# Where the two parts of a weight tile lie in a line of 256 bytes: a two-block transformer on one Trainium2 core

## What is computed

```python
def swiglu(h, w_in, w_out):                 # w_in 1024 x 5632, w_out 2816 x 1024
    gate, up = jnp.split(h @ w_in, 2, axis=-1)
    return (jax.nn.silu(gate) * up) @ w_out

def first_block(x, c, ctx, ...):            # 2 layers: layer 0 differential, layer 1 grouped attention
    for i in range(DEPTH):
        h = half_ffn(h, ...);  hc = half_ffn(hc, ...)            # gated residual of swiglu
        y, yc = mixer(modulated_norm(h, ...), modulated_norm(hc, ...))   # q, k, v = split(t @ w_in)
        h = gated_residual(h, y, ...);  h = half_ffn(h, ...)     # hc too, in layer 0
    return h

def hybrid_layer(x, w_in, ...):             # second_block: 2 of these
    p = rms_norm(x, norm_w) @ w_in          # three branches: sparse attention, stick breaking, mLSTM
    ...                                     # sb_v and ml_v are among the columns of p
    mixed = jnp.sum(gates * jnp.einsum('bsgc,gcd->bsgd', branches, w_branch), axis=2)
    return x + mixed @ w_out
```

## The kernel before

| half | high part | low part | the activation |
|---|---|---|---|
| product with 512 columns | 64 | 64 | 64 (moves) |
| product with 256 columns | 0 | 128 | 64 (moves) |
| value tile | 0 (moves) | 128 (moves) | 64 (stationary) |

## Time and profile before

### The profile page before, as it was taken

One profiled execution on the slowest core, in us unless ns is written; L12 is line 12 of the kernel. 1 busy time (PEld: TensorE's weight loads), 2 busy tenths in 40 slices (PEclk: granted clock), 3 DMA queues, 4 the chain that ended last, 5 costly groups with the idle time before them and its releaser, 6 DMA issues.

```text
span 2405.2 us, 36353 instructions
## 1 busy us (share of the span) xinstructions
PE 2367.2 (98%) x14712; PEld 2054.0 (85%) x14712; DVE 1599.4 (66%) x2899; ACT 1063.0 (44%) x1882; POOL 0.2 (0%) x4
## 2 busy tenths in 40 slices
PE   9999999999999999999999999999999999999998
PEld 5888888976688888888888888899999998999997
DVE  7777775477677677377623367655686776876767
ACT  4222325355552223252223256644556556555563
POOL 0000000000000000000000000000000000000000
PEclk9999999999999999999999999999999999999999
DMA  6554551211125455215522212345543533444432
GB/s 278 206 202 184 210 193 71 88 53 53 65 98 195 190 199 204 89 59 206 213 100 102 91 71 88 112 175 193 193 143 131 192 124 140 169 156 162 154 123 88
DMA packets 48408, 346.53 MB, mean 144 GB/s; under 512 B 5361, under 2 KB 5489, under 8 KB 6769
## 3 DMA queue, kind: packets, MB, share of 16 engines
q1 hardware_dynamic: 48242, 344.21, 38.4%
HBM read 343.14 MB, written 1.05 MB: 143 GB/s over the span
## 4 chain that ended last, share of the span: by engine, by line
PE 90%; DVE 6%; ACT 2%; issue 1%; DMA 0%; DVEq 0%; SPq 0%; ACTq 0%
PE ps L502 25%; PE ps L503 25%; PE ps L504 25%; DVE w_lo L2137 1%; PE ps L844 1%; PE ps L846 1%; PE ps L845 1%; PE ps L891 1%; PE ps L1048 1%; ACT w_hi L1448 1%; PE ps L672 1%; PE ps L697 1%; PE ps L1074 1%; PE ps L877 1%; DVE small L2415 1%
## 5 line engine op out<-in xcount | busy, mean ns | idle before, releaser
L1448 ACT ACTIVATE w_hi<-ring 128x1024 fp32r<-128x1024 f32 x494 | 523.9, 1061 | 1040.0 <-PE ps L504 971.6
L2137 DVE TENSOR_TENSOR w_lo<-ring,w_hi 128x1024 fp32r<-128x1024 f32 x494 | 603.1, 1222 | 422.4 <-ACT w_hi L1448 420.4
L502 PE MATMUL ps<-u_hi,w_hi 128*128 128x512 f32 (+1 forms) x1856 | 654.4, 353 | 4.8 <-DVE u_lo L2210 2.3
L503 PE MATMUL ps<-u_lo,w_hi 128*128 128x512 f32 (+1 forms) x1856 | 644.0, 347 | 0.0
L504 PE MATMUL ps<-u_hi,w_lo 128*128 128x512 f32 (+1 forms) x1856 | 643.6, 347 | 0.0
L502 PEld LDWEIGHTS ps<-u_hi,w_hi 128*128 128x128 f32 x1856 | 348.5, 188 | 57.1 <-issue 7.8
L504 PEld LDWEIGHTS ps<-u_hi,w_lo 128*128 128x128 f32 x1856 | 348.3, 188 | 45.7
L503 PEld LDWEIGHTS ps<-u_lo,w_hi 128*128 128x128 f32 x1856 | 348.5, 188 | 44.5 <-issue 0.5
L502 PE MATMUL ps<-uh,w_hi 128*128 128x256 f32 x1136 | 321.7, 283 | 4.0 <-DVE w_lo L2137 2.6
L2125 DVE CUSTOM_DVE_ANT_0 waste<-ring,condb,cols 128x1024 f32<-128x1024 f32 x260 | 322.2, 1278 | 0.1
L503 PE MATMUL ps<-ul,w_hi 128*128 128x256 f32 x1136 | 317.3, 279 | 0.0
(11 more groups left out here) (364 smaller groups left out, 2679.5 us busy)
## 6 DMA issues: line engine op xcount, KB each, us to landing
ring<-in_wk SPq DMA_DIRECT2D x317, 1024.0 KB, 4.8
mix<-in_wk SPq DMA_DIRECT2D x3, 1024.0 KB, 15.1
yT<-in_wk SPq DMA_DIRECT2D x2, 1024.0 KB, 5.9
hT<-in_x SPq DMA_DIRECT2D x1, 2048.0 KB, 11.3
htabs<-in_htabs SPq DMA_DIRECT2D x1, 1088.0 KB, 7.0
out_t<-uT SPq DMA_DIRECT2D x2, 512.0 KB, 2.6
trig<-in_trig SPq DMA_DIRECT2D x3, 256.0 KB, 7.2
wuk<-in_uk SPq DMA_DIRECT2D x2, 256.0 KB, 5.0
```

Of the source, the lines that this page charges most:

```text
L502: mm(bank, hi, x_hi, start=first, stop=False, skip_group_check=skip)
L503: mm(bank, hi, x_lo, start=False, stop=False, skip_group_check=skip)
L1448: f(half_hi(K, 0, HALF), ringed(n, K % 2 * HALF, (K % 2 + 1) * HALF), ACT.Copy).then_inc(whi_ready, 1)
L2137: tt(half_lo(K, 0, HALF), ringed(HALF_SLOT[K], K % 2 * HALF, (K % 2 + 1) * HALF), half_hi(K, 0, HALF).bitcast(F32), ALU.subtract).then_inc ...
```

## The change

The table has a letter for each half in place of a yes or no: `w` for products with 512 columns, `n` for those with 256, `v` for value tiles. Two kinds of half change their place:

- `w` (512 columns): high part at 64 as before, low part at 192 instead of 64, that is 128 bytes further on than the high part. The distances between the stationary weight and the moving activation within the three matmuls are then 0, 0 and 128 bytes; as each weight load runs beside the matmul ahead of it, the sequence of load against running matmul is 0, 128, 0 (the high part again beside the first, the low part beside the second, the next high part beside the third). Before it was 0, 0, 0.
- `v` (value tiles): high part at 0 as before, low part at 0 instead of 128.
- `n`: unchanged, 0 and 128.

`w_lo` gets 64 bytes longer at its end, and hT, cols, tabs, htabs, trig and the small arrays move up by 64 bytes (tabs from 0 to 64 past a multiple of 256). `phases` is rounded up to the same address as before, so no activation array of the products moves. No instruction is added, removed or put elsewhere on any engine, and no wait changes; only start addresses do.

```diff
-def wide_halves():
-
-    middle = [True] * (FT - NW) + [False] * NW
-    ffn = [False] * 3 + [True] * (2 * FT - 3) + middle
-    da = [False] * (3 + DA_HEADS) + [True] * (2 * DA_HEADS - 3) + [True] * ADDED + [False] * NW
-    first = [True] * (2 * FT) + middle + da + ffn + ffn
-    return first + [False] * (HALVES - len(first))
+def half_kinds():
+
+    middle = "w" * (FT - NW) + "n" * NW
+    ffn = "nnn" + "w" * (2 * FT - 3) + middle
+    da = "nnn" + "v" * DA_HEADS + "w" * (2 * DA_HEADS - 3) + "w" * ADDED + "n" * NW
+    ga = "n" * 10 + "vv" + "n" * KC
+    second = "n" * 16 + "vvvv" + "n" * 8 + "vvvv" + "n" * 60
+    return "w" * (2 * FT) + middle + da + ffn + ffn + ga + "n" * (3 * FT) + second * DEPTH
...
-WIDE = wide_halves()
+HALF_KIND = half_kinds()
+assert len(HALF_KIND) == HALVES
 
 LINE = 256
 NARROW_APART = 64
-ASIDE = NARROW_APART // 4
-LOW_ASIDE = LINE // 2 // 4
+HIGH_AT = dict(w=64, n=0, v=0)
+LOW_AT = dict(w=192, n=128, v=0)
 HALF_PITCH = HALF + LINE // 4
...
-        w_lo = place("fixed", "w_lo", (NW - 1) * HALF_PITCH + HALF + LOW_ASIDE, F32R)
+        w_lo = place("fixed", "w_lo", (NW - 1) * HALF_PITCH + HALF + max(LOW_AT.values()) // 4, F32R)
...
         def half_hi(h, a, b):
-            n = (h % NW) * HALF_PITCH + (ASIDE if WIDE[h] else 0)
+            n = (h % NW) * HALF_PITCH + HIGH_AT[HALF_KIND[h]] // 4
             return w_hi[:, n + a:n + b]
 
         def half_lo(h, a, b):
-            n = (h % NW) * HALF_PITCH + (ASIDE if WIDE[h] else LOW_ASIDE)
+            n = (h % NW) * HALF_PITCH + LOW_AT[HALF_KIND[h]] // 4
             return w_lo[:, n + a:n + b]
```

## The result

| | before | changed |
|---|---|---|
| median of the timed runs, us | 2413.44 (4 runs, 2408.53 to 2418.47) | 2436.28 (4 runs, 2432.51 to 2438.25) |
| ratio to before | | 1.0091, 95% interval 1.0075 to 1.0108 |
| span of the profiled execution, us | 2405.2 | 2436.5 |

The change costs 23 us, 0.9%. The profiled execution of the changed kernel is its slowest of the four (2438.25 us whole), that of before a quick one (2406.99), so the two profiles lie 31.3 us apart and not 23. The page of the changed kernel answers to the earlier trace rows: span, busy time, clock, chain.

What follows compares the result with a forecast made beforehand. PE, busy 98% of the span, bounds the kernel through matmul count times start distance. Terms -3.9 - 2.1 - 0.3 = -6.3 us took the profiled 2407.0 to 2400.7, or 2404.2 on the median's scale; range 2397 to 2430.

Steps and rivals of the forecast that it cites:

- 512-column products, low part at 192: 4824 matmuls of 512-column products: best -1.1 us, worst 26.5 us loss, taken as -0.3 us.
- The sign of being wrong that the prediction names: Wrong in sign if the 512-column windows lose more than a few matmuls; the first must keep 1413.
- Rival A: 512-column products leave their floor as the stationary operand jumps 128 bytes: 2415 to 2433, middle 2424; chance 0.28.
- Value tiles: 864 value-tile matmuls go from 117.8 to 113.3 ns with a steady 64-byte distance: -3.9 us.
- Rival C: Value tiles get worse from a standing clash at 64 bytes, slow spacing handed on: 2414 to 2416; chance 0.07.
- The forecast of 282 matmuls from 433 to 465 us: Sign in the value-tile window: about 282 matmuls in place of 274 if value tiles reach 113.3 ns.
- What follows the value tiles: 16 columns of 24 matmuls after the value tiles, each layer: between 0 and -4.2 us, taken as -2.1.
- a spacing that is handed on: Projections starting without pause after value tiles inherit their spacing; floor handed on saves 2.1 us per layer.
- The shift: 64 bytes of shift in tabs and the small arrays: under 0.5 us, taken as 0.
- Rival B: Addresses don't decide the spacing; how an engine enters a stretch does: time stays 2410.5; chance 0.18.

Runs made afterwards that it cites:

- e2: Against the kernel before, only the 512-column low part moved to 192, with w_lo 64 bytes longer; 2432.98 us, ratio 1.0089.
- e4: Against the kernel before, both parts of the 512-column halves at 192, w_lo 64 bytes longer, value tiles unchanged; 2440.21 us, ratio 1.0118.
- e11: Against the kernel before, 256-column halves at 64 and 192, value tiles both at 0, w_lo 64 bytes longer; 2426.36 us, ratio 1.0047.
- e7: Against the kernel before, 512-column halves at 0 and 128 with activations still at 64; 2436.62 us, ratio 1.0095.
- e1: Against the kernel before, only the value tiles' low part moved to 0, nothing behind w_lo shifted; 2405.62 us against 2412.1, ratio 0.9973.
- e9: Against the kernel before, both parts of the 256-column halves at 0 and both parts of the value tiles at 128; 2412.98 us, ratio 0.9994.
- e6: Against the kernel before, value tiles have both parts at 64, distance 0 from the activation; 2410.75 us, ratio 0.9990.
- e3: Against the kernel before, all halves unmoved, only w_lo 64 bytes longer so later arrays move up; 2411.86 us, ratio 1.0000.
- e12: Against the kernel before, 256-column high and low parts exchanged (128 and 0), value tiles both at 0; 2397.07 us against 2414.49, ratio 0.9924.

## Why the prediction was wrong

The forecast was 2404, the measured time 2436, above the range's end of 2430. Against before's median of the same session (2413.4) the change is +23 us where -6.3 was forecast.

*The step that failed: "512-column products, low part at 192", taken as -0.3 us.* It measured +19.9 us in the profile (1.5 to 21.4 over the floor), and e2 shows it alone: +0.9%. The sign of being wrong that the prediction names came: the first 512-column window lost 26 of its 1413. My two reasons for the small number both failed. The first was that the 256-column form, with the same 128 bytes between its parts, holds the floor through 973 matmuls, "so a stationary operand that jumps by 128 need not cost anything". But the step between the parts is not the whole matter (e4 has none and is slower than the changed kernel). The distance from the load to the running matmul matters too: it is 128 here for the low part, and the 256-column form has 64 there, never 128, so its row could not stand for this pattern. The second was that a longer matmul can take up more. It does so at distances 0, 128, 0 only in part (4.4 ns each with 512 columns, 5.8 with 256 in e11), and 64 bytes to either side shows the reverse (e7: up to 6.7 ns each, more than the 5.6 of the 256-column form). Rival A had the sign, the persistence ("a slow state would be kept") and the size (8.8 to 26.5 us), but its reason, the jump of the stationary operand alone, is not enough by e4. It got 0.28. The distance of 128 had no row in the trace at all. For a place with nothing to gain and 26.5 us to lose, and no row for it, the likelier value was not the one at the good end.

*Value tiles, taken as -3.9 us.* The direction was right, the size too large: -2.3 us in the changed kernel's profile. They reach the floor, as in the fourth window, but in about half of their stretches; a steady pair at 64 bytes has two spacings (e1, e9), and the comparison with the steady 512-column pair did not hold, as that has distance 0. Rival C is out. The forecast of 282 matmuls from 433 to 465 us left out the 2.4 under way at the edge; at the floor it would be 285.

*What follows the value tiles, taken as -2.1 us.* In the changed kernel 0: both stretches of 16 columns stayed at 118.8. In e1 and e6 it was the whole 4.2. But the reason given, a spacing that is handed on, does not hold in general: in e6 slow value tiles are followed by the floor, and in e9 the value tiles just ahead are at the floor and the 16 columns (45 in the 5 us from 1905) are not.

*The shift, taken as 0.* Right on the clock: e3 has ratio 1.0000.

*Not priced: 256-column stretches that change their spacing.* They make up 10.7 us of the profile's 31.3, 5.7 of them in one stretch. I had named the two spacings and taken the change between them as a saving only. What part of the 10.7 belongs to the change is not settled: the timed median rose by 23 and not 31 us, and e3 has the same slow stretch at no cost in its median. The profile of before was one of its quick executions, and that of the changed kernel its slowest.

*Rival B, that addresses don't matter,* is out: ratios run from 0.9924 to 1.0118 with nothing but start addresses changed. Half of it holds: at the same places a 256-column stretch can take either of two spacings. The page behind it, the Trainium skill's "SBUF — State Buffer", section "Who interferes with whom", says that PE's two read ports are independent and that PE never waits on anyone. Read as "no address matters", that is contradicted by these fp32r products; whether the ports are what gets in the way, no run shows.

What stays open: what the chip does at each distance, what a step between loads adds with 512 columns, and what sets the spacing at which a stretch starts. No trace shows an address or a read.

## What to carry to other kernels

Where TensorE streams products without a pause, measure the distance between starts per form, and compare it with the lowest that the form reaches anywhere; 2 to 5% can hide there in a page that shows PE 98% busy. Then try the places of the stationary operand against the moving one within 256 bytes, for each width by itself: what is free at one width was the worst at another. And price a pattern that the trace doesn't contain by its worst neighbour, above all where the best it can do is nothing.

## What the runs showed of the hardware that I had not expected

Time over the floor per matmul in fp32r products, each with a weight load of 128 x 128 ("+64": the load's operand 64 bytes beyond the moving one; from the distances of starts in the long stretches). The order is that of load beside the first, second and third matmul.

| distances | 512 columns, floor 226.7 ns | 256 columns, floor 113.3 ns |
|---|---|---|
| 0, 0, 0 | 0 | 6.7 |
| 0, 128, 0 | 4.4 | 5.8 |
| 128, 128, 128 | 5.7 | not run |
| -64, +64, -64 | 2.2 or 6.7 | 0 or 5.6 |
| -64, -64, -64 | not run | 0 or 4.4 |
| +64, +64, +64 | not run | 0 or 4.4 (4.4 in the long stretches read) |
| +64, -64, +64 | not run | 0, back to it from every start in the trace |
| value tiles: 0 / 128 / steady 64 / two at +64, one at -64 | | 6.7 / 5.3 / 0 or 4.4 / 4.4 |

The distances in their order are not the whole rule. Value tiles of before meet +64, +64, -64, and the 256-column halves of e12 meet +64, -64, +64, the same round begun elsewhere. Yet the first are 4.4 ns over the floor in all their stretches in seven profiles, and the second find back to it. What differs is which operand steps by 128 bytes: the moving one in value tiles, the stationary one in e12. No run takes the two apart further.

Most of the numbers are whole steps: 6.67 ns is 16 cycles of the 2.4 GHz clock for each matmul, 4.44 is 32 cycles for three, 2.22 is 16 for three, 5.56 is 40 for three, and the floor itself is 17 cycles for 16 columns at either width. The values 5.3, 5.7 and 5.8 ns are not.
